# New orders of work in the first block of a three-block network, on TensorE, ScalarE, VectorE and the DMA queue

## What is computed

```python
mod = jax.nn.silu(c) @ w_ada[l] + b_ada[l]                  # 1024 x 6144: twelve tiles of 512 columns
h = rmsnorm(x, g_pre_mix[l]) * (1.0 + scale_m) + shift_m
proj = h @ w_in[l]                                          # 1024 x 3072: six tiles of 512 columns
rq, rk, rv, rg, aq, ak, av = jnp.split(proj, split_at, axis=-1)
y_ret = bidirectional_retention(...)                        # then normed and gated by silu(rg)
y_att = ...                                                 # softmax attention of 8 heads
mixed = jnp.concatenate([y_ret, y_att], axis=-1) @ w_out[l] # 1024 x 1024: two tiles
x = x + gate_m * rmsnorm(mixed, g_post_mix[l])
h = rmsnorm(x, g_pre_ffn[l]) * (1.0 + scale_f) + shift_f
moe = expert_choice_moe(h, w_router[l], w_gate_e[l], w_up_e[l], w_down_e[l])   # 16 experts, 32 tokens each
x = x + gate_f * rmsnorm(moe, g_post_ffn[l])
```

## Time and profile before

| | us |
|---|---|
| median of 3 runs (lowest to highest) | 2329.12 (2320.78 to 2334.85) |
| the profiled execution, its own time | 2326.23 |
| its span, first to last instruction | 2324.4 |
| PE busy over the span | 2018.8 (87%) |
| DVE, ACT busy over the span | 1017.9 (44%), 728.8 (31%) |
| mean granted TensorE clock | 0.909 |

### The profile page before, as it was taken

One profiled execution on the slowest core, in us unless ns is written; L12 is line 12 of the kernel. 1 busy time (PEld: TensorE's weight loads), 2 busy tenths in 40 slices (PEclk: granted clock), 3 DMA queues, 4 the chain that ended last, 5 costly groups with the idle time before them and its releaser, 6 DMA issues.

```text
span 2324.4 us, 30721 instructions
## 1 busy us (share of the span) xinstructions
PE 2018.8 (87%) x12679; PEld 1488.4 (64%) x12680; DVE 1017.9 (44%) x1136; ACT 728.8 (31%) x799; POOL 28.3 (1%) x23
## 2 busy tenths in 40 slices
PE   8897877777776777767689999999999999999999
PEld 6677433333333333333378899998888889998887
DVE  5563000000000000000177786877777768777776
ACT  3442100000000000000144446544444444745443
POOL 0000000000000000000000002000000000200000
PEclk9997878777787887788899999999999999999999
DMA  9675799999999999999945565455565566545554
GB/s 354 217 279 223 317 429 429 429 429 429 429 429 428 429 429 429 429 429 428 408 137 186 156 209 181 153 197 193 152 212 182 159 184 208 180 149 200 181 159 132
DMA packets 233161, 657.03 MB, mean 283 GB/s; under 512 B 6948, under 2 KB 121956, under 8 KB 208484
## 3 DMA queue, kind: packets, MB, share of 16 engines
q1 hardware_dynamic: 233060, 655.62, 73.7%
HBM read 654.54 MB, written 1.05 MB: 282 GB/s over the span
## 4 chain that ended last, share of the span: by engine, by line
issue 85%; PE 13%; DVE 1%; POOL 1%; ACT 0%; DVEq 0%; POOLq 0%; ACTq 0%
PE psum L1212 3%; PE psum L1213 2%; PE psum L1234 2%; PE psum L1235 2%; PE psum L1236 2%; PE psum L1313 2%; PE psum L1314 1%; DVE ring_r L2139 1%; PE psum L1280 0%; POOL work L739 0%; ACT ring_r L1614 0%; POOL work L738 0%; PE psum L1281 0%; POOL work L740 0%; DVE x L2435 0%
## 5 line engine op out<-in xcount | busy, mean ns | idle before, releaser
L2139 DVE TENSOR_TENSOR ring_r<-ring,ring_r 128x2048 fp32r<-128x2048 f32 (+2 forms) x182 | 452.7, 2518 | 101.7 <-ACT ring_r L1614 101.0
L1212 PE MATMUL psum<-work_r,ring_r 128*128 128x512 f32 x1280 | 450.5, 397 | 3.1 <-DVE ring_r L2139 3.1
L1614 ACT CAST ring_r<-ring 128x2048 fp32r<-128x2048 f32 (+2 forms) x180 | 360.4, 2043 | 291.8 <-PE psum L1314 122.3
L1213 PE MATMUL psum<-work_r,ring_r 128*128 128x256 f32 x1280 | 358.3, 280 | 0.0
L1129 PE MATMUL psum<-ring,work 128*32 128x512 f32 x1536 | 213.8, 695 | 106.0 <-DMA ring<-in_w_up_e_dram 106.0
L1212 PEld LDWEIGHTS psum<-work_r,ring_r 128*128 128x128 f32 x1280 | 240.4, 188 | 62.5 <-issue 3.7
L1234 PE MATMUL psum<-work_r,ring_r 128*128 128x256 f32 x928 | 263.3, 284 | 2.5 <-DVE ring_r L2139 2.5
L1235 PE MATMUL psum<-work_r,ring_r 128*128 128x256 f32 x928 | 262.2, 283 | 0.0
L1236 PE MATMUL psum<-work_r,ring_r 128*128 128x256 f32 x928 | 261.9, 282 | 0.0
L1313 PE MATMUL psum<-work_r,ring_r 128*128 128x512 f32 x704 | 248.2, 398 | 2.9 <-DVE ring_r L2139 2.9
L1213 PEld LDWEIGHTS psum<-work_r,ring_r 128*128 128x128 f32 x1280 | 241.4, 189 | 0.0
(11 more groups left out here) (301 smaller groups left out, 2304.5 us busy)
## 6 DMA issues: line engine op xcount, KB each, us to landing
ring<-in_w_up_e_dram SPq DMA_DIRECT2D x64, 2048.0 KB, 25.3
work<-in_w_down_e_dram SPq DMA_DIRECT2D x48, 2048.0 KB, 31.6
ring<-in_ffn_w_up_dram SPq DMA_DIRECT2D x41, 2048.0 KB, 7.9
work<-in_w_gate_e_dram SPq DMA_DIRECT2D x32, 2048.0 KB, 11.2
ring<-in_w_gate_e_dram SPq DMA_DIRECT2D x32, 2048.0 KB, 14.3
ring<-in_w_in_dram SPq DMA_DIRECT2D x25, 2048.0 KB, 8.5
ring<-in_ffn_w_down_dram SPq DMA_DIRECT2D x32, 1408.0 KB, 6.9
ring<-in_w_down_e_dram SPq DMA_DIRECT2D x16, 2048.0 KB, 34.9
```

What stands on the lines that cost most here:

```text
L1212: pe.matmul(dst, w_hi[:, k, cols], h_both(k), start=(k == 0), stop=False)
L1213: mm = pe.matmul(dst[:, 0:S], w_lo[:, k, cols], h_hi_[:, S * k:S * (k + 1)], start=False, stop=(k == KD - 1))
L1614: act.copy(hi_unit(name, unit), raw_unit(name, unit)).then_inc(hi_ready, 1)
L2139: dve.tensor_tensor(lo_unit(name, unit), raw_unit(name, unit), hi_unit(name, unit).bitcast(F32), ALU.subtract).then_inc(lo_ready, 1)
```

## The change

Five things are changed, all in the first block:

1. The order of the calls on PE, ACT and DVE between `head_tile` and the output projection. `split_first` is called for one unit at a time.
2. The order of the loads: each win and wout tile is issued ahead of one ada tile that stood ahead of it.
3. The small loads: the rows of the second layer now stand behind win 4, and the router's weights behind win 5, with a semaphore of their own (`router_loaded`).
4. PE turns the layers' rows ahead of `head_tile` instead of behind it.
5. Slot 8 is given back ahead of the last 96 matmuls of the output projection, slot 4 after 72 of them, slot 5 behind them as before. `EXPERT_SLOTS` is changed to go with that: up 0 to 3 take slots 8, 0, 4, 1 and down 0 takes slot 5.

The number of instructions that compute is the same. The diff, with the lists on PE, ACT and DVE shown at their beginnings:

```diff
@@ -102,13 +102,13 @@
 
 
     order = [("ada", 0), ("ada", 1), ("ada", 2), ("ada", 3), ("win", 3), ("win", 4), ("ada", 4), ("ada", 5), ("win", 5),
-             ("ada", 6), ("win", 0), ("ada", 7), ("win", 1), ("ada", 8), ("win", 2), ("ada", 9), ("wout", 0),
-             ("ada", 10), ("wout", 1), ("ada", 11)]
+             ("win", 0), ("ada", 6), ("win", 1), ("ada", 7), ("win", 2), ("ada", 8), ("wout", 0), ("ada", 9),
+             ("wout", 1), ("ada", 10), ("ada", 11)]
     return [(name, 1, 0 if name[0] == "ada" else 2, first_slot(*name)) for i, name in enumerate(order)]
 
 
 
-EXPERT_SLOTS = (6, 7, 2, 3, 0, 1, 4, 5, 8)
+EXPERT_SLOTS = (6, 7, 2, 3, 8, 0, 4, 1, 5)
 LAYER_SLOTS = (0, 2, 1, 3)
 
 
@@ -467,6 +467,7 @@
         slot_granted = sem("slot_granted")
...
@@ -587,18 +588,14 @@
                 src = a[name][0] if name != "final_norm" else a[name]
                 sp.dma_start(rows_in[fo[name]:fo[name] + n, 0, :], src.rearrange("(c p) -> c p", p=P)).then_inc(rows_loaded, 16)
 
-            def small_loads():
-                for i, name in enumerate(("ret_decay_fwd", "ret_decay_bwd")):
-                    sp.dma_start(decay_in[:, 4 * i:4 * i + 4], a[name].to_broadcast([P, 4])).then_inc(misc_loaded, 16)
-                for l in range(LAYERS):
-                    for name, n in LAYER_ROWS:
-                        src = a[name][l]
-                        if name == "conv_w":
-                            src = src.rearrange("k (c p) -> (k c) p", p=P)
-                        elif name not in ("lru_b_a", "lru_b_x", "pool_b"):
-                            src = src.rearrange("(c p) -> c p", p=P)
-                        sp.dma_start(rows_in[lo[name]:lo[name] + n, 1 + l, :], src).then_inc(layer_rows_loaded, 16)
-                sp.dma_start(w_router[:], a["w_router"][0].rearrange("(k p) e -> p k e", p=P)).then_inc(misc_loaded, 16)
+            def layer_rows(l):
+                for name, n in LAYER_ROWS:
+                    src = a[name][l]
+                    if name == "conv_w":
+                        src = src.rearrange("k (c p) -> (k c) p", p=P)
+                    elif name not in ("lru_b_a", "lru_b_x", "pool_b"):
+                        src = src.rearrange("(c p) -> c p", p=P)
+                    sp.dma_start(rows_in[lo[name]:lo[name] + n, 1 + l, :], src).then_inc(layer_rows_loaded, 16)
 
             def pair_half(i, half):
 
@@ -622,7 +619,13 @@
                 else:
                     load(name, slot_view(name, KD, 512), columns(w, 512 * i, 512))
                 if name == ("win", 3):
-                    small_loads()
+                    for i, small in enumerate(("ret_decay_fwd", "ret_decay_bwd")):
+                        sp.dma_start(decay_in[:, 4 * i:4 * i + 4], a[small].to_broadcast([P, 4])).then_inc(misc_loaded, 16)
+                    layer_rows(0)
+                if name == ("win", 4):
+                    layer_rows(1)
+                if name == ("win", 5):
+                    sp.dma_start(w_router[:], a["w_router"][0].rearrange("(k p) e -> p k e", p=P)).then_inc(router_loaded, 16)
 
             with sp.Fori(0, E) as e:
 
...
@@ -963,50 +966,50 @@
                                        start=(s == 0), stop=(s == TT - 1), skip_group_check=True)
                 mm.then_inc(att_done, 1)
 
+            layer_columns()
             head_tile()
+            win_unit(2)
             modulation(4)
-            layer_columns()
-            win_unit(2)
+            win_unit(3)
             modulation_columns(4)
-            win_unit(3)
+            att_scores(0)
             modulation(5)
-            att_scores(0)
             win_unit(4)
             modulation_columns(5)
             win_unit(5)
+            att_scores(1)
             att_transpose(0)
-            att_scores(1)
+            modulation(6)
             win_unit(6)
-            modulation(6)
             att_transpose(1)
             win_unit(7)
             att_values(0)
             att_transpose(2)
+            modulation_columns(6)
             att_scores(2)
-            modulation_columns(6)
             win_unit(8)
+            win_unit(9)
...
@@ -1040,7 +1043,7 @@
                                   skip_group_check=True)
                         mm = pe.matmul(out_c, w_lo[:, k, cols], mixin_hi[:, tokens], start=False,
                                        stop=(closes and k == ks[-1]), skip_group_check=True)
-                if closes:
+                if closes and 3 in blocks:
                     mm.then_inc(tile_done[ring_plan.slot(name)], 1)
 
             pe.wait_ge(mixin_lo_ready, 1)
@@ -1057,10 +1060,14 @@
             wout_products(1, (2, 3), (4, 5, 6, 7), opens=True)
             modulation_columns(11)
             pe.wait_ge(mixin_lo_ready, 4)
-            for i in range(2):
-                wout_products(i, (0, 1, 2, 3), (0, 1, 2, 3), closes=True)
-            for s in (4, 5, 8):
-                pe.sem_inc(tile_done[s], 1)
+            pe.sem_inc(tile_done[8], 1)
+            wout_products(0, (0, 1, 2, 3), (0, 1, 2, 3), closes=True)
+            wout_products(1, (0, 1), (0, 1, 2, 3), closes=True)
+            pe.wait_ge(tile_done[0], ring_plan.done(("wout", 0)))
+            pe.sem_inc(tile_done[4], 1)
+            wout_products(1, (2, 3), (0, 1, 2, 3), closes=True)
+            pe.wait_ge(tile_done[1], ring_plan.done(("wout", 1)))
+            pe.sem_inc(tile_done[5], 1)
 
             square_sums(sq_ready, 5, 5, ms_done)
             spread_columns(rstd_ready, 2, bank[5], TT, rstd_spread)
@@ -1068,7 +1075,7 @@
             spread_columns(rstd_ready, 3, bank[5], TT, rstd_spread)
 
 
-            pe.wait_ge(misc_loaded, 48)
+            pe.wait_ge(router_loaded, 16)
             for k in range(KD):
                 pe.wait_ge(h_ready, KD + k + 1)
                 for t in range(TT):
...
             evict(0)
+            soft_exp()
             evict(1)
-            soft_exp()
-            split_first(("win", 5))
             evict(2)
+            split_first(("win", 5), (0,))
+            split_first(("win", 5), (1,))
             evict(3)
-            split_first(("win", 0))
             att_softmax(0)
+            att_weights(0)
+            split_first(("win", 0), (0,))
             att_softmax(1)
+            decay_exp(0)
             evict(4)
-            att_weights(0)
+            evict(5)
+            att_softmax(2)
+            split_first(("win", 0), (1,))
             att_weights(1)
-            evict(5)
             att_copy(0)
             split_first(("win", 1), (0,))
-            att_softmax(2)
+            att_weights(2)
+            split_first(("win", 1), (1,))
+            att_copy(1)
+            evict(6)
             att_softmax(3)
-            evict(6)
-            att_copy(1)
-            split_first(("win", 1), (1,))
+            att_weights(3)
             evict(7)
-            att_weights(2)
-            att_copy(2)
...
@@ -1899,7 +1910,7 @@
                                          bank[5][:, S + P * l:S + P * l + n_layer]))
                 step(dve.tensor_copy(layer_cols[:, LAYERS * n_layer:], first_cols[:, fo["final_norm"]:fo["final_norm"] + KD]))
                 dve.tensor_copy(ident_r[:], ident[:]).then_inc(ident_r_ready, 1)
-                dve.wait_ge(misc_loaded, 48)
+                dve.wait_ge(misc_loaded, 32)
                 for l in range(LAYERS):
                     at = n_layer * l + lo["lru_lambda"]
                     step(dve.tensor_copy(decay_in[:, 8 + HEADS * l:8 + HEADS * (l + 1)], layer_cols[:, at:at + HEADS]))
...
 
+            layer_columns()
+            layer_constants()
             modulation(4)
-            layer_columns()
-            split_first(("win", 5))
+            split_first(("win", 5), (0,))
             modulation_columns(4)
-            layer_constants()
+            split_first(("win", 5), (1,))
+            att_scores(0)
+            decay_log(0)
+            modulation(5)
+            att_sums(0)
+            modulation_columns(5)
+            att_scores(1)
             split_first(("win", 0), (0,))
-            modulation(5)
-            att_scores(0)
-            att_scores(1)
-            split_first(("win", 0), (1,))
-            modulation_columns(5)
-            att_sums(0)
             att_sums(1)
             att_scores(2)
             att_scores(3)
+            att_sums(2)
+            split_first(("win", 0), (1,))
+            modulation(6)
+            decay_log(1)
             split_first(("win", 1), (0,))
-            modulation(6)
             split_first(("win", 1), (1,))
-            att_sums(2)
             att_sums(3)
+            att_scores(4)
             modulation_columns(6)
-            att_scores(4)
             att_scores(5)
+            decay_log(2)
+            values_centred(0)
             split_first(("win", 2), (0,))
```

97 lines of the change are left out of this document (47 added, 50 removed).

## The result

| | before | after |
|---|---|---|
| median of 10 runs each, us | 2329.28 (2320.78 to 2335.42) | 2315.03 (2312.14 to 2323.62) |
| ratio of the times, 95% interval | | 0.994 (0.9923 to 0.9957) |
| profiled execution: time, span, us | 2326.23, 2324.4 | 2314.14, 2312.3 |
| end of the warming products | 36.19 | 38.17 |
| head tile, start to end | 37.28 to 49.03 | 41.67 to 55.01 |

14 us faster by the medians, 0.6%: forecast were 2316 and a gain of 13.4 us. The interval of the ratio leaves 10 to 18 us. The stages behind the first block keep their lengths. From the first gate product to the end of the span it is 2324.4 - 239.04 = 2085.4 us before and 2312.3 - 228.4 = 2083.9 after, and from the closing products' end to the gate product 47.0 us in both. So the gain lies ahead of the closing products. There the profiled execution doesn't add up as the sum did, though.

What follows compares the result with a forecast made beforehand. PE was taken as the bound from 37 to 192 us, ahead of DMA-bound experts. Terms -10.6 - 5.0 - 0.2 + 0.6 + 1.8 = -13.4 us took the profiled 2326.2 to 2312.8, median 2316; range 2309 to 2329.

Steps and rivals of the forecast that it cites:

- Where the time is set: First block: the kernel's end moves by what the end of the output projection, at 192 us, moves.
- Waits, -10.6: Five PE waits between head tile and closing products (2.00, 2.29, 2.04, 0.73, 3.53 us) all go: -10.6 us.
- Clock, -5.0: PE's half-clock stretches after the waits around 75 and 140 us go with the idle time: -5.0 us.
- the third dip: PE's clock at 0.57 from 164 to 168 us, without a gap; its 1.7 us loss was left in.
- Head tile, -0.2 and +0.6: Ahead of the head tile: transposes move into a 1.09 us wait, -0.2; second layer's rows land behind win 4, +0.6.
- New waits, +1.8: Steps with little to spare on PE's new path may wait: between 0 and 5 us, taken as +1.8.
- the three near misses: Steps with little to spare: unit 4 (0.4 us), retention scores (0.9), spread of the group norms (1.1).
- What costs nothing: Swapped loads, later router weights, slots given back earlier and two added PE waits: no effect on the time.
- (a): Rival, PE in the first block: low clock stays or waits come back in part; about 2321 us, chance 0.30.
- (b): Rival: waits only move along the heads' chain, or the norm chain gives the gain back; 2329 us, chance 0.14.
- (c): Rival, ahead of the head tile: second layer's rows land at 51.9 us, head tile 14.6 late; 2330 us, chance 0.06.
- Signs: Trace readings named beforehand, from 37 us to the first gate product, to show the forecast right or wrong.

Runs made afterwards that it cites:

- the second profile: The changed kernel, unaltered, run and profiled again beside later runs on the same chip: 2316.48 us, ratio 0.994.
- the first of these experiments: The changed kernel with TensorE turning the layers' rows behind the head tile again, as in the kernel before: 2310.22 us, ratio 0.9908.

## Why the prediction was right, point by point

**The number.** That the median came within 1 us of 2316 is luck in part: the interval leaves 10 to 18 us, the profiled pair moved by 12.1, and two terms of the sum were off in opposite directions.

**Where the time is set.** Right. The closing products' end moved by 10.58 us, the first gate product by 10.64 and the span by 12.1, with the distance between the first two unchanged at 47.0 us.

**Waits, -10.6.** Right: none of the five is left, in any of the executions of the changed kernel.

**Clock, -5.0.** Right, and shown apart from the waits: with the gaps kept and filled it came back, 6.2 us with the third dip. That I left the 1.7 us of this dip in held in both profiles of the changed kernel. But it isn't tied to the order of products: it is in nine of the twelve profiles in which the products stand in that order, and missing in three. The rule of the Trainium skill that I had weighed ("TensorE: Matmul & The Clock Gate", "What's actually happening") would have given 1.7 us more; it fits the runs where the gaps are filled, and fails at 152 to 160 us, where PE was busy and read 0.82 and 0.76.

**Head tile, -0.2 and +0.6.** This is the term that was mis-sized. I let the last bytes of win 4 land at about 36.5 us and the rows shortly behind, so that the head tile starts at 37.3 to 38.8; it started at 41.67 and 41.50. The step that failed is the landing of the big tile itself. Its issue in the changed kernel, and below it its row in the list of issues (what, KB, us from issue to landing):

```profile
29.51 0.40 SPq L580 DMA_DIRECT2D ring<-in_w_in_dram  x1
```

```profile
ring<-in_w_in_dram SPq DMA_DIRECT2D x1, 2048.0 KB, 10.0
```

It was issued when I said (3.8 us earlier than in the kernel before) and landed at 39.5, in the second profile at 29.24 + 9.9 = 39.1: some 3 us late. My 36.5 gave it 7 us, where the shortest of the earlier trace rows is 8.7. The rows released TensorE 1.9 and 2.1 us behind it (41.38 and 41.21), and the head tile started 2.2 and 2.4 us behind it, about the 2.3 that my latest start, 38.8, had allowed. The gap ahead of the head tile grew by 2.4 us in one profile and by 4.3 in the other (41.50 - 36.13 - 1.09), and I had not costed what the clock does behind it: the head tile took 1.6 and 1.4 us more than in the earlier trace rows's execution, which was a lucky one: in four more profiles with the old orders it took 13.20, 13.05, 13.03 and 11.74 us. Moving the rows or their columns off the path gave back 4 to 6 us in the medians, more than the traces account for (2.8 and 4.4 us for the first of these experiments).

**New waits, +1.8.** Did not come. From 48 to 152 us PE has no idle time; the three near misses (0.4, 0.9 and 1.1 us) all held. In the profiled pair the head tile cost 3.6 us more than forecast (4.0 against 0.4), and the stretch behind it gained 2.8 us more (16.6 against 13.8), which is why the total fits better than its terms. The upper end of 5 us that I gave this term doesn't follow from its own words: half of the first two waits is 2.1 us.

**What costs nothing.** The give-back: no run shows a worth. That win 4 and the rows of the second layer change places held for the slots; its price stands under the head tile. The order of the tiles' loads had no term of its own, only the remark that win units come sooner by it. Alone it shows no gain, but with the new lists it is needed, and turning it back costs some 20 us by the two ratios.

**The rivals.** (a) did not happen between the head tile and the closing products, where no window is at 0.50; the one at 0.50 (40 to 44 us) is the head tile's. (b) neither: 181.44. (c) happened in part: its sign, a wait above 2.5 us ahead of `head_tile`, was there with 3.22, and the experiment with later rows confirmed its price at the point where it decides.

**Signs.** The closing products were to end at about 178.5 and the gate product to start near 225.5: they came 2.9 us later, 2.0 of it the prologue's. The clock at 76 to 84 and 144 to 150 us was 1.00 as said. PE was to be idle for less than 2 us from 37 us on; the one wait was 3.22, so this sign was missed.

## What to carry to other kernels

An order of work and an order of loads are one thing where an engine takes its instructions strictly in order: placing a conversion at its tile's landing is right only while that landing keeps its place, and what a late tile costs is read from what is queued behind the conversion, not from who needs the tile. A gap of TensorE costs its length and can cost a stretch at half clock behind it (here 5.0 us behind gaps of 2.29 and 3.53, nothing behind two of 2.0), so look for both in the windows. Where a gap can't be removed, products that nobody reads can save the second part if they are no longer than the gap: here they gave 0.3% (0.1 to 0.5), and nothing where they were 1 and 2 us too long. What lands behind a big tile is forecast from that tile's own time from issue to landing, as rows of the same stretch show it. Transfers of a few KB that an engine will wait for belong ahead of a 2 MB tile in the queue, or their users behind the next big block of work.

## What the runs showed that I had not expected

- Small rows queued behind a 2 MB tile released their user 7.6 and 7.7 us after the last issue (33.77 to 41.38, 33.54 to 41.21), later ones behind two more tiles 8.9 us, those ahead of the tile 5.1 us.
- The same prologue ends between 33.1 and 38.2 us in executions of kernels whose work on TensorE doesn't differ there, in part because a stretch around one modulation group is at low clock in some of them (0.57 from 28 to 32 us in the changed kernel, where the group takes 3.55 us instead of 1.92). These 5 us are part of the 20 us over which times of the kernel before range, and a reason why two traces should be compared from the warming products' end.
- The clock fell where PE was busy all the time with one-column products and 128x128 transposes between longer ones, in nine of twelve profiles (one or two windows of 4 us at 0.57 to 0.91, which cost 1.7 us in each), and not at all in the others.
